# Column form for keys, values and gates; value products on alternating column halves; the token gathers spread over two queues

## The reference

```
proj = rms_norm(x) @ w_in                  # columns: 3328 RWKV | 1024 queries | 6 x 256 keys/values | 48 gates
q, cmp_kv, slc_kv, win_kv = ...            # three [key, value] pairs of 4 heads x 64
gates = sigmoid(proj[..., last 48])        # 3 branches x 16 query heads
o_cmp, sel_idx = cmp_attend_select(q, compress(cmp_kv), ...)   # 31 compressed blocks in the prompt, 255 per sampled token
o_slc = slc_attend(q, ..., sel_idx, ...)   # 16 selected blocks of 64 rows, per token and kv head
o_win = window_attend(q, win_kv)           # 512 last positions
nsa = gates[0] * o_cmp + gates[1] * o_slc + gates[2] * o_win
x = x + concat(rwkv_out, nsa) @ w_o        # then the FFN, and a final norm
```

## Time and profile before

| | us |
|---|---|
| median of three runs | 3827.37 |
| lowest, highest | 3818.47, 3828.94 |
| the profiled execution | 3826.18 |
| its span, first to last instruction | 3824.3 |

### The profile page before, as it was taken

The page is one execution under the profiler, slowest core; times in us unless marked ns, Lnnn a source line. Parts: engine busy times, 40 slices in busy tenths (PEclk is TensorE's granted clock), DMA queues, the critical chain, the costliest instruction groups (busy, mean ns, idle before and its releaser), DMA issues. The chain is left out here.

```text
span 3824.3 us, 69061 instructions
## 1 busy us (share of the span) xinstructions
PE 3480.3 (91%) x29822; PEld 3146.9 (82%) x29822; DVE 1401.0 (37%) x1775; ACT 1014.9 (27%) x1410; POOL 484.1 (13%) x536
## 2 busy tenths in 40 slices
PE   7999999569968999679968989999999999999998
PEld 6999999348847777443326989999999999999997
DVE  4222220653345665135533233333333333333334
ACT  4111110533314665124312231221221122122112
POOL 2000000353423333300000000000000000000000
PEclk8999998569978999769988999999999999999999
DMA  6433331565626442523252323333333333333332
GB/s 180 116 113 110 97 87 40 172 188 132 161 50 243 191 192 83 173 92 74 50 176 83 88 74 93 89 91 97 89 89 89 99 90 89 90 98 89 89 94 95
DMA packets 506389, 423.91 MB, mean 111 GB/s; under 512 B 144613, under 2 KB 458454, under 8 KB 501518
## 3 DMA queue, kind: packets, MB, share of 16 engines
q1 hardware_dynamic: 481630, 302.76, 28.1%
q0 software_dynamic: 15392, 115.99, 8.3%
q10 hardware_dynamic: 9136, 1.72, 0.2%
HBM read 381.94 MB, written 65.76 MB: 117 GB/s over the span
## 5 line engine op out<-in xcount | busy, mean ns | idle before, releaser
L2760 DVE TENSOR_TENSOR f_w_lo<-wo_raw,f_w_hi 128x2048 fp32r<-128x2048 f32 x132 | 302.5, 2292 | 815.2 <-ACT f_w_hi L2732 815.2
L53 PE MATMUL d_ps<-hh,f_w_hi 128*128 128x260 f32 x2816 | 567.5, 283 | 11.3 <-DVE f_w_lo L2760 11.3
L57 PE MATMUL d_ps<-hh,f_w_lo 128*128 128x260 f32 x2816 | 568.4, 284 | 0.0
L55 PE MATMUL d_ps<-hl,f_w_hi 128*128 128x260 f32 x2816 | 567.6, 283 | 0.0
L2732 ACT CAST f_w_hi<-wo_raw 128x2048 fp32r<-128x2048 f32 x132 | 252.0, 1909 | 1005.6 <-DMA wo_raw<-in_w_gate 413.7
L53 PEld LDWEIGHTS d_ps<-hh,f_w_hi 128*128 128x128 f32 x2816 | 435.2, 189 | 11.7 <-DVE f_w_lo L2760 11.7
L57 PEld LDWEIGHTS d_ps<-hh,f_w_lo 128*128 128x128 f32 x2816 | 435.1, 189 | 0.0
L55 PEld LDWEIGHTS d_ps<-hl,f_w_hi 128*128 128x128 f32 x2816 | 433.8, 189 | 0.0
L53 PE MATMUL d_ps<-f_hid_hi,f_w_hi 128*128 128x260 f32 x1408 | 283.9, 283 | 4.2 <-DVE xt L2784 4.0
L57 PE MATMUL d_ps<-f_hid_hi,f_w_lo 128*128 128x260 f32 x1408 | 283.4, 283 | 0.0
L55 PE MATMUL d_ps<-f_hid_lo,f_w_hi 128*128 128x260 f32 x1408 | 282.5, 282 | 0.0
(11 more groups left out here) (453 smaller groups left out, 5861.3 us busy)
## 6 DMA issues: line engine op xcount, KB each, us to landing
p_w<-in_w_in SPq DMA_DIRECT2D x46, 1024.0 KB, 5.6
wo_raw<-in_w_gate SPq DMA_DIRECT2D x44, 1024.0 KB, 5.7
wo_raw<-in_w_up SPq DMA_DIRECT2D x44, 1024.0 KB, 5.7
wo_raw<-in_w_down SPq DMA_DIRECT2D x44, 1024.0 KB, 5.1
wo_raw<-in_w_o SPq DMA_DIRECT2D x16, 1024.0 KB, 5.9
sel_d<-in_cache_slc_kv SPq DMA_DIRECT2D x364, 32.0 KB, 2.1
rk_chunks<-r_outb POOLq DMA_DIRECT2D x8, 1280.0 KB, 6.2
s_cur<-rk_chunks SPq DMA_DIRECT2D x8, 1280.0 KB, 7.0
```

What stands on the lines that cost most here:

```text
L53: pe.matmul(out[j], w_hi, x_hi[j], start=start, stop=False)
L55: pe.matmul(out[j], w_hi, x_lo[j], start=False, stop=False)
L57: last = pe.matmul(out[j], w_lo, x_hi[j], start=False, stop=stop)
L2760: dve.tensor_tensor(w_lo[:, s, :], w_raw[:, s, :], w_hi[:, s, :].bitcast(F32), ALU.subtract).then_inc(lo_done, 1)
```

## The change

- Input projection: keys, values and gates are computed in column form too, as units 34 to 46 (the gates are unit 35), with 260 tokens to a bank; the eight query units also drop to 260. PE then turns each unit (`turn`: five transposes), and DVE or ACT copies the rows out. The keys of the selected and window branch are also stored by columns, in a new `k_t`. The loops are written out, and loads of weights wait for the low part instead of the products.
- Prompt attention: `kT` is loaded from `k_t`, `kvr` shrinks to the values `vr`, the turning of keys on PE and its eight copies go, and the two loads come behind `qT`.
- `values` takes two blocks at a time: the even block on one half of the array's columns, the odd one on the other, in matmuls of 256 tokens that alternate (512 in the first pair of a tile). Each half sums its blocks. ACT copies one half to `other`, DVE adds the two into `mo`. `pT` has four buffers.
- Gathers: SP takes tokens 0 to 4, POOL 5, 6 and 7, all in the prompt attention; ACT issues none. `mix_ahead` moves behind token 5 on POOL, and the stores of `mo` stand between the later gathers. POOL's clearing of semaphores moves ahead of all of these.

```diff
 def stage_in_proj(nc, g):
...
+                def columns(u):
+                    s, w, bank, n = u % 4, width(u), 2 * (u % 3), wide(u)
+                    pe.wait_ge(lo_done, u + 1)
+                    if u >= 3:
+                        wait_copied(pe, u - 3)
                     for k in range(KT):
...
+                def turn(u):
+                    s, n = u % 4, wide(u)
+                    wait_copied(pe, u)
+                    if u > CU:
+                        pe.wait_ge(row_copied, u - CU)
+                    for t in range(4):
+                        pe.transpose(ps[:, 6, t * n:(t + 1) * n], ob[0:n, s, t * P:(t + 1) * P], g.ident[0:n, 0:n])
+                    pe.transpose(ps[0:NB, 7, 0:n], ob[0:n, s, SEQ:TC], g.ident[0:n, 0:n]).then_inc(turned, 1)
+
+                for u in range(UN):
+                    columns(u)
+                    if u > CU:
+                        turn(u - 1)
+                turn(UN - 1)
...
+                    elif in_columns(u):
+                        r = key_row(u)
+                        pool.dma_start(g.k_t[r:r + P, :], ob[:, s, 0:SEQ]).then_inc(stored[s], 16)
 def stage_nsa_picked(nc, g):
...
-                regs = [act.alloc_register(f"last_place{n}") for n in range(4)]
-                with nc.allow_non_contiguous_dma(reason="small tables"):
-                    places_in(act, g, adr_row, adr_in)
-                gather(act, g, adr_row, regs, NB - 1, range(4))
 def stage_nsa_prompt(nc, g):
...
-                for t in range(NQ):
-                    sp.dma_start(kvr[:, t, :], g.kv_rows[t * P:(t + 1) * P, 512:1536]).then_inc(kv_in[t], 16)
...
+                for br in range(2):
+                    for h in range(2):
+                        sp.dma_start(kT[half(h), :, br, :], g.k_t[br * 256:(br + 1) * 256].rearrange("(i d) t -> d i t", d=C)).then_inc(
+                            k_in, 16)
+                for br in range(2):
+                    sp.dma_start(vr[:, :, br, :], g.kv_rows[0:SEQ, 768 + 512 * br:1024 + 512 * br].rearrange(
+                        "(t p) n -> p t n", p=P)).then_inc(v_in, 16)
...
-                mix_ahead(pool, g)
...
+                clear_old(pool, g)
...
+                gather(pool, g, late_row, regs, SP_TOKENS, range(4))
+                mix_ahead(pool, g)
+                gather(pool, g, late_row, regs, SP_TOKENS + 1, range(4))
+                store(0)
+                gather(pool, g, late_row, regs, SP_TOKENS + 2, range(2))
+                store(1)
+                gather(pool, g, late_row, regs, SP_TOKENS + 2, range(2, 4))
+                store(2)
+                store(3)
...
+                    pe.wait_ge(ptd, n0 // 2 + 1)
+                    pe.wait_ge(pta, n0 // 2 + 1)
+                    for cols in ((slice(0, SEQ),) if begin else (slice(0, SEQ // 2), slice(SEQ // 2, SEQ))):
+                        for n in (n0, n0 + 1):
+                            u, j = blocks[n]
+                            br = units[u][2]
+                            last = pe.matmul(ps[half(n + 1), bank, cols], vr[:, j, br, i * C:(i + 1) * C], pT[:, n % 4, cols],
+                                             start=begin and n == n0, stop=False, skip_group_check=True)
...
-                        if n >= 2:
-                            values(n - 2)
+                        if n >= 3 and n % 2:
+                            values(n - 3)
...
+                    act.copy(other[half(i), :], ps[half(i + 1), 6 + m % 2, :]).then_inc(other_kept, 1)
...
+                    dve.tensor_tensor(mo[half(i), :, t * P:(t + 1) * P],
+                                      ps[half(i), 6 + m % 2, :].rearrange("p (q t) -> p q t", q=4),
+                                      other[half(i), :].rearrange("p (q t) -> p q t", q=4), ALU.add).then_inc(o_kept, 1)
```

More of the change, by code:

```diff
@@ L267, in slot, with sem @@
[L267 to L279, removed]
-                              ALU.subtract).then_inc(lo_done, 1)
+        def sem(name):
+            return new_sem(nc, g, "p_" + name)
@@ L284, in _ @@
             def _(sp):
[L285 to L303, removed]
+                for u in range(UN):
+                    s, n = u % 4, wide(u)
+                    if u >= 4:
+                        sp.wait_ge(lo_done, u - 3)
+                    sp.dma_start(w_raw[:, s, :, 0:n], w_view[:, :, cols(u)]).then_inc(loaded[s], 16)
@@ L319, in rows @@
[L319 to L327, removed]
@@ L376, in _, with sigmoid @@
+                copy_rows(dve, UN - 1, dve.tensor_copy)
             @block.scalar
             def _(act):
+                def sigmoid(out, in_):
+                    return act.activation(out, in_, ACT.Sigmoid)
                 for u in range(2):
-                    high(act, 0, u)
-                with act.Fori(0, quads) as i:
-                    for s in range(4):
-                        high(act, i, s + 2)
-                        if s % 2 == 1:
-                            copy_columns(act, i, s, act.copy)
@@ L396, in _ @@
+                for u in range(UN):
+                    if u + 2 < UN:
+                        high(act, u + 2)
+                    if u % 2 == 1:
+                        copy_out(act, u, sigmoid if u == GU else act.copy, copied_a)
+                    if u - 1 >= CU and u % 2 == 0:
+                        copy_rows(act, u - 1, act.copy)
             @block.gpsimd
             def _(pool):
-                def store_columns(i, s):
-                    pool.wait_ge(copied[s], i * 2 + 2)
-                    pool.dma_start(g.proj_t[bass.ds(i * 512 + s * P, P), :], ob[:, s, :]).then_inc(stored[s], 16)
@@ L418, in _ @@
+                for u in range(UN):
+                    columns_out(u)
+                    if u == GU + 2:
+                        pool.wait_ge(row_copied, 2)
+                        store_rows(grow, g.gates, NG, gates_stored)
+                    if u >= CU + 4 and (u - CU) % 2 == 0:
+                        rows_out((u - CU - 4) // 2)
+                rows_out(KU // 2 - 1)
                 for s in range(4):
-                    pool.wait_ge(stored[s], 16 * (quads + (s < 2)))
+                    pool.wait_ge(stored[s], stores_of(s, UN))
@@ L2218, in _ @@
                 gather(sp, g, adr_row, regs, 0, (2, 3))
[L2219 to L2220 removed]
+                for b in range(1, SP_TOKENS):
+                    if b == 3:
                         wo_ahead(sp, g)
```

286 lines of the change are left out of this document (139 added, 147 removed).

## The result

The changed kernel takes 3729.0 us (median of four, 3727.1 to 3738.0) where the kernel before took 3824.8 beside it: a ratio of 0.9756, 95% interval 0.9733 to 0.9778. On a second chip it was 0.9741 (0.9719 to 0.9762). The forecast was 3730 with a range of 3712 to 3768. The profiled execution took 3727.2 us, its span is 3725.6.

A forecast was written before the change was run, and what follows sets the result against it. PE alone bounds the projection; in attention PE also waits for ACT and DVE, and SP's gathers end the stage. From 3826.2 us, -47.9 - 21 - 13 - 2.3 - 12.9 = -97.1 gives 3729.1, forecast 3730, range 3712 to 3768.

The forecast's parts named there:

- 1, column form: Input projection: keys, values and gates in column form save PE 50.9 us, a longer end costs 3; together -47.9 us.
- 2, loads: Start of prompt attention: queries loaded ahead of keys and values land by 1621.4 instead of 1642.4; -21 us, bounds -12 and -24.
- 3, value products: Prompt attention: paired value products on overlapping column halves; -13 us after 11 for the lower clock, bounds -20 and +10.
- 4, end of the stage: End of prompt attention: SP's gathers stop being last, PE's end plus copy, add, store and landing takes 6.9 us; -2.3 us.
- 5, GpSimd's gathers: Prompt attention: POOL's 156 gathers at 1.1 us each end at about 1800, under the attention; price 0.
- 6, picked blocks: Picked blocks: without gathers on ACT, PE's 12.93 us wait behind its exponential goes; -12.9 us.
- A: Prompt attention: PE, idle more, may stay at 1.2 GHz; kernel 3860 if fully (chance 0.02), 3745 to 3775 if partly (0.12).
- B: Prompt attention: POOL's gathers are slow; 3740 to 3810 at 1.6 to 2.3 us each (chance 0.12), beyond 2.4 us 0.02.
- C: Prompt attention: the column halves do not overlap in one bank, pairs take 2.0 us; kernel 3747, chance 0.06.
- D: Start of prompt attention: queries still land late because of small pieces ahead of them; -10 instead of -21, kernel 3741, chance 0.08.
- E: Input projection: column form costs more, by dearer transposes and end or a slow gate unit; +10 to +15, 3742, chance 0.08.

The follow-up runs named there:

- Experiments 2 to 5: Kernel before rerun (chunks 268.1 us) and with 128 idle PE waits (267.2); changed kernel, last store on SyncE, with 128 or 64 waits: ratios 0.9717, 0.9721.
- experiment 7: Changed kernel with value products one after the other on one column half, as before; ratio to the kernel before 0.9773, prompt attention stage 319.0 us for 296.5.
- experiment 10: Changed kernel with gathers as before: SyncE tokens 0 to 6, ScalarE the last, GpSimd none and loading the residual first; ratio to the kernel before 0.9886.
- Experiment 6: Changed kernel with the last store of the prompt attention on SyncE in place of GpSimd; ratio to the kernel before 0.9733, stage 290.2 us for 296.5.

## Why the prediction was right, and where it was not

**1, column form: -47.9, measured -51.7, and +7 it did not have.** The mechanism held. PE gained 53.4 us instead of 50.9, because a matmul took 0.118 us and not 0.120: 840 instructions in 100 us, of which 41 belong to the turns of 8.2 units. The end grew by 1.7 us, not 3. Left out was what a stage costs other stages: its code is longer and PE's later code stands elsewhere, and the chunks stage pays some 7 us (12.4 between the two first traces). Experiments 2 to 5 make the place of PE's code the likely cause of most of it: with 128 waits the gaps stand elsewhere and the stage is within 1 us of the four old ones' mean, 268.0. That rests on one trace for each place.

**2, loads: -21, measured -18.9.** PE's scores came 12.4 us after the stage's first load, forecast 10 to 11. The sum counted queries alone on the DMA engines, so it had both causes in it; the text named the keys and values first, and the residual was the larger one, four to one.

**3, value products: -13, measured -24.2** (250.9 to 226.7 us), outside its range. The mechanism held, as experiment 7 shows: without the pairing the attention takes 250.7 us. Its size was off in three places. I let the two instructions of one matmul follow each other on one half and got five steps of 0.25 us a pair; the trace has four, 1.0 us. With four, the order written out gives 223.9 us for 227.1, by my own sum. The order itself was too slow where PE waits for copies: pass (2, 1) was to grow from 9.2 to 9.8 us, and in the traces it falls from 9.06 to 8.72; the last pass of a head takes 5.55 us at full clock, 7.81 before, and I had 6.4 for a pass with 128-token scores behind four blocks. And on top of an order that was too long I added 11 us for the lower clock. What the clock takes of the 226.7 us is not shown as a whole. It is more than the 2.8 us that are left over 223.9: the last two passes of the first head alone took 3.1 us longer at 0.80 than those of the second head at 1.00. The kernel of experiment 10 did the whole attention in 223.4 us and that with the residual early in 231.3:

```profile
1642.01:1865.43 223.42, 191.58 (x993) 102.25 (x992) 144.09 (x343) 97.99 (x313) 1.89 (x3) 0.92 0.25 58
1640.91:1872.22 231.31, 201.74 (x993) 108.20 (x992) 144.73 (x343) 98.19 (x313) 57.71 (x98) 0.87 0.29 64
```

The Trainium skill ("TensorEngine Tiling (Array Packing)", section "Overview") promises up to 2x for two halves of 64 columns; the pairs show just that.

**4, end of the stage: -2.3, measured +5.8.** From PE's last matmul (ends at 1853.5) to the next stage it is 15.7 us, forecast 6.9. SyncE stopped being last, as forecast. The step that failed is "POOL's store and its landing": the landing took 4.3 us, and then GpSimd kept the stage for 9 more. Experiment 6 takes these away. What GpSimd waited for is open.

**5, GpSimd's gathers: 0, measured 0, but for 3.5 us that are counted under step 4.** They cost 0.70 us each and not 1.1. All the same the last came later than forecast, 204 us after the stage's start (1777.0 - 1572.6) for 189 (1800 - 1611.1): the last 52 stand behind stores that wait for finished heads, and the sum had left that out. DVE never waited for a store. The Trainium skill ("SBUF — State Buffer", section "SBUF: two separate sides") tells of a GpSimd DMA that went from 620 to 3100 ns beside a copy of VectorE; nothing like it is in this trace, where the longest of the 156 took 0.735 us beside a DVE that was busy 64% of the attention.

**6, picked blocks: -12.9, measured -17.** The first traces overstate it by some 3 us: the seven with ScalarE's gathers average 102.9 us, the seven without 88.5, a difference of 14.4.

The errors nearly cancel: -3.8 in step 1, -11.2 in step 3 and -4.1 in step 6 against +2.1, +8.1 and the chunks' +12.4; the other -5.1 lie in stretches that no step speaks of. So the total came within 1 us by luck: it did not show that the terms were right. Of the rivals, A, B and C did not happen. D did in part: PE's first scores came 1.4 to 2.4 us later than forecast; that the small pieces did it is not shown. E's dearer transposes did not come.

## What to carry to other kernels

When one engine stops being last in a stage, look at who closes it: here moving one store from GpSimd to SyncE was worth 6 us of the stage. A load that is not needed for 100 us can cost its whole transfer time if it is issued beside one that PE waits for. And when a stage that was not touched gets longer, look for gaps put down to issue inside runs of equal instructions: the code may merely stand in another place.

## What the runs showed of the hardware

- In the chunks stage PE stood idle for up to 3.1 us without a wait that the profile shows, in 76 of 85 cases from 0 to 2.4 us after a load of a code block had started, though most of the 47 loads of a stage have no such gap; behind some gaps the granted clock stood at 0.50 for 3.4 to 14 us. With the code moved by 128 instructions the gaps stood elsewhere and the stage took 268.7 us for 274.8, in one trace each.
- Value matmuls on alternating column halves of one PSUM bank overlap fully: eight instructions of 256 columns in 1.0 us, where one half alone took 2.0.
- A stage that GpSimd closes with a store of 512 KB ends 13.8 us after the issue (10.3 in the kernel where GpSimd issued no gathers between its stores); with the same store on SyncE 4.8 us.
- Gathers of 32 KB cost GpSimd 0.70 us each with their registers, SyncE 0.90 and ScalarE 0.95 to 1.01.
- The best kernels of the study are the changed one with the last store on SyncE and 64 or 128 idle waits: 3717.0 and 3720.0 us, which their intervals do not tell apart, beside 3730.6 for the changed kernel.
